# Turning the FFN's gated product on VectorE and by SBUF transfers instead of on TensorE

## The reference

```python
h2 = rms_norm(x, g_pre_ffn[l]) * (1 + scale_f) + shift_f
f = (jax.nn.silu(h2 @ w_ffn_gate[l]) * (h2 @ w_ffn_up[l])) @ w_ffn_down[l]
x = x + gate_f * rms_norm(f, g_post_ffn[l])
```

## Time and profile before

| | before |
|---|---|
| time, median of 3 runs | 2398.11 us (2397.22 to 2399.67) |
| span of the profiled execution | 2395.4 us |
| mean granted TensorE clock | 0.999 |
| PE, busy share of the span | 99% |
| DVE, busy share | 67% |
| ACT, busy share | 47% |
| POOL, busy share | 0% |
| FFN, gate and up product | about 698 to 1163 us of the span |

### The profile page before, as it was taken

The page is one execution under the profiler, slowest core; times in us unless marked ns, Lnnn a source line. Parts: engine busy times, 40 slices in busy tenths (PEclk is TensorE's granted clock), DMA queues, the critical chain, the costliest instruction groups (busy, mean ns, idle before and its releaser), DMA issues.

```text
span 2395.4 us, 31219 instructions
## 1 busy us (share of the span) xinstructions
PE 2379.1 (99%) x11027; PEld 1973.6 (82%) x11027; DVE 1594.5 (67%) x1962; ACT 1120.6 (47%) x1415; POOL 9.8 (0%) x18
## 2 busy tenths in 40 slices
PE   8999999999999999999999999999999999999998
PEld 7888788888888888888888888888888888888887
DVE  7998899899787765444444465446654557777664
ACT  4544545544464444444444454445544444444554
POOL 0001000000000000000000000000000000000000
PEclk9999999999999999999999999999999999999999
DMA  9986479999768875555655555655555554444454
GB/s 392 384 313 209 155 265 352 331 343 366 294 202 273 281 245 192 188 180 197 207 193 193 193 193 180 210 201 184 201 192 187 183 194 158 148 167 155 157 190 159
DMA packets 148490, 539.32 MB, mean 225 GB/s; under 512 B 16768, under 2 KB 18080, under 8 KB 147744
## 3 DMA queue, kind: packets, MB, share of 16 engines
q1 hardware_dynamic: 145584, 528.28, 64.4%
q10 hardware_dynamic: 2800, 9.59, 1.1%
HBM read 535.69 MB, written 2.11 MB: 225 GB/s over the span
## 4 chain that ended last, share of the span: by engine, by line
PE 98%; DVE 1%; DMA 1%; ACT 0%; issue 0%; SPq 0%; ACTq 0%; DVEq 0%
PE acc L1970 29%; PE acc L1972 29%; PE acc L1971 29%; PE tb L2052 2%; PE tb L2509 1%; DMA start_raw<-in_wa_dram 1%; PE tb L1970 1%; PE tb L1971 0%; PE tb L1972 0%; PE acc L2022 0%; PE acc L2021 0%; PE acc L2020 0%; PE tb L2512 0%; PE tb L2239 0%; PE acc L2031 0%; DVE macc L1340 0%
## 5 line engine op out<-in xcount | busy, mean ns | idle before, releaser
L1149 DVE TENSOR_TENSOR lo<-raw,hi 128x1024 fp32r<-128x1024 f32 x809 | 968.2, 1208 | 596.8 <-ACT hi L566 595.0
L566 ACT ACTIVATE hi<-raw 128x1024 fp32r<-128x1024 f32 x809 | 842.1, 1049 | 900.4 <-PE acc L1972 705.5
L1970 PE MATMUL acc<-hi,Hh 128*128 128x512 f32 x1960 | 775.4, 396 | 1.2 <-DVE Hl L1692 0.7
L1972 PE MATMUL acc<-hi,Hl 128*128 128x512 f32 x1960 | 764.3, 390 | 0.0
L1971 PE MATMUL acc<-lo,Hh 128*128 128x512 f32 x1960 | 763.1, 389 | 0.0
L1970 PEld LDWEIGHTS acc<-hi,Hh 128*128 128x128 f32 x1960 | 368.1, 188 | 79.0 <-issue 4.4
L1972 PEld LDWEIGHTS acc<-hi,Hl 128*128 128x128 f32 x1960 | 367.9, 188 | 77.7
L1971 PEld LDWEIGHTS acc<-lo,Hh 128*128 128x128 f32 x1960 | 368.4, 188 | 75.5 <-issue 1.4
L1970 PE MATMUL acc<-hi,hbh 128*128 128x512 f32 x512 | 204.8, 400 | 0.0
L1972 PE MATMUL acc<-hi,hbl 128*128 128x512 f32 x512 | 200.1, 391 | 0.0
L1971 PE MATMUL acc<-lo,hbh 128*128 128x512 f32 x512 | 199.6, 390 | 0.0
(11 more groups left out here) (325 smaller groups left out, 1966.5 us busy)
## 6 DMA issues: line engine op xcount, KB each, us to landing
raw<-in_wa_dram SPq DMA_DIRECT2D x680, 512.0 KB, 4.3
late_raw<-in_wa_dram SPq DMA_DIRECT2D x96, 512.0 KB, 5.4
raw<-in_wb_dram SPq DMA_DIRECT2D x96, 512.0 KB, 3.4
start_raw<-in_wa_dram SPq DMA_DIRECT2D x64, 512.0 KB, 7.8
raw<-in_wc_dram SPq DMA_DIRECT2D x64, 512.0 KB, 4.2
x<-in_x_dram SPq DMA_DIRECT2D x2, 1024.0 KB, 6.1
gm<-gate_rows ACTq DMA_DIRECT2D x2, 1024.0 KB, 8.2
x<-in_x_dram ACTq DMA_DIRECT2D x1, 2048.0 KB, 9.2
```

Of the source, the lines that this page charges most:

```text
L566: act.activation(hi[:, s, 0:n], raw[:, r, 0:n], ACT.Copy).then_inc(hi_ready, 1)
L1149: dve.tensor_tensor(lo[:, s, 0:n], raw[:, r, 0:n], hi[:, s, 0:n].bitcast(F32), ALU.subtract)\
L1970: pe.matmul(dst(tt), a, hi[:, s, w], start=first and i == 0, stop=False)
L1972: mm = pe.matmul(dst(tt), b, hi[:, s, w], start=False, stop=last and i == kts - 1)
```

## The change

The product in `tok` is no longer turned by PE. DVE turns the 32 x 32 blocks of each token tile (two `STREAM_TRANSPOSE` instructions from `tok` into `sgt`), which leaves each block in the wrong group of 32 partitions. POOL then issues sixteen SBUF to SBUF transfers of 32 partitions x 256 float32 (32 KB, rows of 1 KB), one for each pair of groups, from `sgt` back into `tok`. ACT and DVE take `hidh` and `hidl` from `tok` instead of from `tb`, in `hidden_hi` and `hidden_lo`. All of it waits on four new semaphores: `hid_blocks` (DVE to POOL), `hid_turned` (the transfers to ACT, 256 for each hidden tile), `hid_hi` (ACT to DVE), `hid_split` (DVE to PE, before the down product's first unit and before its unit 20).

```diff
+        blocks_out = sgt[:].rearrange("p a (j m) -> p (a j) m", j=2)
+        blocks_in = tok[:, 0].rearrange("p a (i m) -> p (a i) m", i=2)
+        def turned_half(tt):
+            return blocks_in[:, :, tt * P:(tt + 1) * P].rearrange("p i (k t) -> p k i t", k=4)
...
@@ gpsimd
+            for n in range(FT):
+                pool.wait_ge(hid_blocks, n + 1)
+                for i in range(4):
+                    for j in range(4):
+                        pool.dma_start(blocks_in[32 * j:32 * j + 32, i, :], blocks_out[32 * i:32 * i + 32, j, :])\
+                            .then_inc(hid_turned, 16)
@@ scalar
-            def hidden(n, first=8):
+            def hidden_hi(n, turned):
+                act.wait_ge(hid_turned, turned)
+                for tt in range(TT):
+                    act.activation(hidh[:, cols(n * 4, 4), tt * P:(tt + 1) * P].rearrange("p k (i t) -> p k i t", i=4),
+                                   turned_half(tt), ACT.Copy).then_inc(hid_hi, 1)
+            def hidden(first=5):
                 split(first)
                 tile_done()
                 read_out(lambda tt: sgt[:, tt, :], 0, ACT.Silu)
-                split(8)
-                take_hi_tile(hidh, n * 4)
+                split(11)
...
             for n in range(1, FFN_MOD):
-                hidden(n)
+                hidden_hi(n - 1, 256 * n)
+                hidden()
@@ vector
-            def hidden(n, units=16):
-                split(units - 2)
+            def hidden_lo(n, taken):
+                for tt in range(TT):
+                    dve.wait_ge(hid_hi, taken + tt + 1)
+                    at = slice(tt * P, (tt + 1) * P)
+                    four = lambda ap: ap.rearrange("p k (i t) -> p k i t", i=4)
+                    ins = dve.tensor_tensor(four(hidl[:, cols(n * 4, 4), at]), turned_half(tt),
+                                            four(hidh[:, cols(n * 4, 4), at].bitcast(F32)), ALU.subtract)
+                ins.then_inc(hid_split, 1)
+            def hidden(units=10):
+                split(units)
                 tile_done(2)
                 for tt in range(TT):
                     dve.tensor_tensor(tok[:, 0, tt, :], acc[:, 2 + tt, :], sgt[:, tt, :], ALU.mult).then_inc(acc_free[2 + tt], 1)
-                split(2)
-                take_lo_tile(hidl, hidh, n * 4)
+                n = c.up("hidden")
+                for tt in range(TT):
+                    dve.wait_ge(acc_free[2 + tt], n + (TILES_BEFORE_OUT // 2 + 3))
+                for tt in range(TT):
+                    ins = dve.transpose(blocks_out[:, :, tt * P:(tt + 1) * P].rearrange("p j (k t) -> p j k t", k=4),
+                                        tok[:, 0, tt, :].rearrange("p (k j c) -> p j k c", k=4, j=4))
+                ins.then_inc(hid_blocks, 1)
+                split(6)
@@ tensor
             def next_hidden():
-                def hidden():
-                    read_out(1)
-                    transpose_tok(0, tr_split)
-                tile(Hh, Hl, 0, 8, after={1: hidden})
+                tile(Hh, Hl, 0, 8)
                 tile(Hh, Hl, 1, 8)
...
                 if t == 0:
-                    tile(hidh, hidl, 0, FK // 2, before={FK // 2 - 2: split_now}, after={1: last_hidden})
+                    tile(hidh, hidl, 0, FK // 2, before={i: (lambda n=n: pe.wait_ge(hid_split, n)) for i, n in ((0, FT - 1), (FK // 2 - 2, FT))},
+                         after={1: lambda: gate_rows_out(1)})
```

More of the change, by code:

```diff
@@ L367, in two_blocks @@
         tr_copy = sem("tr_copy")
+        hid_blocks = sem("hid_blocks")
+        hid_turned = sem("hid_turned")
+        hid_hi = sem("hid_hi")
+        hid_split = sem("hid_split")
         uv_summed = sem("uv_summed")
@@ L910, in hidden @@
                 read_out(lambda tt: sgt[:, tt, :], 0, ACT.Silu)
-                split(8)
-                take_hi_tile(hidh, n * 4)
-            hidden(0, FFN0 + 12 - c.n["unit"])
+                split(11)
+            hidden(FFN0 + 12 - c.n["unit"])
             for n in range(1, FFN_MOD):
-                hidden(n)
-            with c.loop(act, FT - FFN_MOD, unit=16, raw=16, split=2) as n:
-                hidden(n + FFN_MOD)
+                hidden_hi(n - 1, 256 * n)
+                hidden()
+            with c.loop(act, FT - FFN_MOD, unit=16, raw=16) as n:
+                hidden_hi(n + (FFN_MOD - 1), n * 256 + 256 * FFN_MOD)
+                hidden()
+            hidden_hi(FT - 1, 256 * FT)
             store_gate(1)
-            split(4)
+            split(1)
             load_gate(gm2, 1)
@@ L1718, in hidden @@
                     dve.tensor_tensor(tok[:, 0, tt, :], acc[:, 2 + tt, :], sgt[:, tt, :], ALU.mult).then_inc(acc_free[2 + tt], 1)
-                split(2)
-                take_lo_tile(hidl, hidh, n * 4)
-            hidden(0, FFN0 + 20 - c.n["unit"])
+                n = c.up("hidden")
[6 more added lines that the diff above has]
+                split(6)
+            hidden(FFN0 + 18 - c.n["unit"])
             for n in range(1, FFN_MOD):
-                hidden(n)
+                hidden_lo(n - 1, TT * (n - 1))
+                hidden()
             add_bias(GATE_F, KD)
             gated_gain(GATE_F, "g_post_ffn")
-            with c.loop(dve, FT - FFN_MOD, unit=16, raw=16, hi=2) as n:
-                hidden(n + FFN_MOD)
+            with c.loop(dve, FT - FFN_MOD, unit=16, raw=16, hidden=1) as n:
+                hidden_lo(n + (FFN_MOD - 1), n * TT + TT * (FFN_MOD - 1))
+                hidden()
+            hidden_lo(FT - 1, TT * (FT - 1))
             for t in range(3):
-                split(FK // 2 - (t == 0))
+                split(FK // 2 - (5 if t == 0 else 0))
                 gated_tile(fmix, gm2, t % 2, t * N)
@@ L2401, in _ @@
                 next_hidden()
-            with c.loop(pe, FT - FFN_MOD, unit=16, raw=16, acc0=1, acc1=1, tb0=1, tb1=1):
+            with c.loop(pe, FT - FFN_MOD, unit=16, raw=16, acc0=1, acc1=1):
                 next_hidden()
[L2405 to L2408, removed]
             for t in range(4):
                 if t == 0:
-                    tile(hidh, hidl, 0, FK // 2, before={FK // 2 - 2: split_now}, after={1: last_hidden})
+                    tile(hidh, hidl, 0, FK // 2, before={i: (lambda n=n: pe.wait_ge(hid_split, n)) for i, n in ((0, FT - 1), (FK // 2 - 2, FT))},
+                         after={1: lambda: gate_rows_out(1)})
                 elif t < 3:
```

## The result

| | before | changed |
|---|---|---|
| time, median of 9 runs | 2397.58 us (2396.95 to 2399.67) | 2403.79 us (2402.63 to 2406.20) |
| ratio to before, 95% interval | | 1.0027 (1.0017 to 1.0036) |
| span of the profiled execution | 2395.4 us | 2404.4 us |
| mean granted TensorE clock | 0.999 | 0.997 |

The change costs 6.2 us, 0.27%. I forecast 2389 us. The page of the changed kernel: span, busy times, the chain that ended last, DMA queues (packets, MB, share), and the new transfers (KB, median us to landing).

What follows compares the result with a forecast made beforehand. PE, busy 99% of the span, was taken to bound the kernel. Span 2395.4 - 9.8 (transposes) + 1.0 (added in tiles 0 to 3) = 2386.6, plus 2.7 for the runs' median, gave 2389 us; range 2386 to 2450.

Steps and rivals of the forecast that it cites:

- the last landing w: Time from the last of POOL's sixteen transfers being issued to its landing; taken as 2 us, 4 beside modulation blocks.
- What bounds the kernel: Claim that the time is the sum of what PE runs: busy 99% of the span, 98% of the last-ending chain.
- what PE gives up: Eight PE transposes per turned hidden tile, claimed to cost 0.89 us; eleven tiles give 9.8 us off the path.
- The deadline: Latest last landing before PE waits for unit 23: 15.5 us after DVE's product starts; 14.6 in tiles 0 to 3.
- T: When a hidden tile's last transfer lands, from the start of DVE's product; forecast 12.7 us, 14.7 in tiles 0 to 3.
- t: Time in us within a hidden tile, counted from the start of DVE's product.
- The issue pitch d: Time between POOL's issues of the sixteen transfers, called the main unknown; taken as 0.5 us, range 0.45 to 1.5.
- S: PE's stall per hidden tile, T - 15.5 us where positive; at 0.89 us it eats up the gain.
- just late: Rival: chain slightly late, pitch 0.70 to 0.75 us or landing 4 us everywhere; 2393 to 2402 us, chance 0.10.
- my last sign of being wrong: Forecast is wrong if DMA load holds the small transfers back by more than 2.8 us over what was taken.
- What else is added: Extra cost of DVE's block transposes ahead of modulation blocks and unit 18 in tiles 0 to 3: 1 us in all.
- a slow issue: Rival: POOL issues the sixteen transfers slowly; at a pitch of 0.9 us the time is 2428 us, chance 0.28.

Runs made afterwards that it cites:

- the kernel with quiet loads: The changed kernel with SP's weight loads from the FFN on cut to a quarter of their width (128 KB instead of 512): 2387.24 us, one run.

## Why the prediction was wrong

I forecast 2389 us and a gain; measured were 2403.79 us and a loss. The step that failed first is the last landing w, which I put at 2 us and which was 5.6. Two more things came on top: I charged too little for what is added in tiles 0 to 3, and I did not foresee a late start of POOL.

**What bounds the kernel, and what PE gives up**: right. The 0.89 us per tile is there, 43.52 us wherever nothing is late, and the kernel turned the new way in seven tiles got 5.4 of the 6.2 us that seven tiles should give.

**The deadline**: right to 0.4 us. I had T = 15.5 for unit 23. Landings at t = 14.9 lost nothing, at 15.1 0.05 us (the kernel with quiet loads, tile 8), at 15.7 0.5, at 15.9 0.8 and at 16.2 1.0, so it lies at 15.1 to 15.2. Part of the difference is the 0.14 us from the landing to `hidh`, which my sum left out.

**The issue pitch d**: I named it the main unknown, took 0.5 us and hung the rivals on it. It was 0.49 us (498 ns for each of 176). The block transposes were as taken too, 1.30 us for the pair. The Trainium skill's 1 us to the first byte ("DMA: Bandwidth & Descriptors", "Latency and other measured facts") was not paid sixteen times: the first transfer of a burst landed 1.7 us after its issue, and the next was issued 0.49 us behind it.

**The last landing w**: this step failed. I took 2 us, for a single small transfer on fairly quiet engines, and 4 for loaded ones only in tiles 0 to 3, from the earlier trace rows. It was 5.6 in tile 7, and 5.2 is the median of all 176. Within the burst of tile 7 the landing grows from 1.7 us for the first transfer to 5.2 for the seventh and stays at 5.2 to 5.9 after that. It takes both the crowd and the loads: beside the full loads one transfer alone lands after 1.7 us, and the last of sixteen after 5.6; with the loads cut to a quarter the last of sixteen lands after 1.7 in tiles 4 to 10.

The trace of the kernel before held nearer rows. Of the five small transfers that gave me the pitch, two are of exactly 32 KB:

```profile
iropeC<-in_table_dram ACTq DMA_DIRECT2D x1, 32.0 KB, 7.5
iropeS<-in_table_dram ACTq DMA_DIRECT2D x1, 32.0 KB, 7.3
```

They were issued one behind another beside loads of about 400 GB/s, and landed after 7.3 to 7.5 us. I took the pitch from this group and not the landing.

The Trainium skill ("DMA: Bandwidth & Descriptors", "Anatomy of one DMA", the GpSimd path) gives a fixed 2.0 us plus the bytes at 436 GB/s; for 32 KB that is 2.1 us, an estimate from that page. The median of the quiet kernel, 2.1, agrees, and that of the change is 3 us above it.

With w = 5.6 my own sum gives T = 1.3 + 1.3 + 0.1 + 8 + 5.6 = 16.3. Measured was 15.9: POOL started at 3.0 and not at 2.7, and the last issue is 15 pitches behind the first, 7.3 us and not 8. So S is 0.8 by my deadline, eleven tiles lose about as much as PE gives up, and the change is close to nothing from these terms. This is the rival that I called "just late" and gave 0.10. It named both ways there, a pitch above 0.7 or a landing of 4 us everywhere, and it was the second; and my last sign of being wrong, small transfers held back by more than 2.8 us over what I took, is what came (3.6 us). The measured time still lies above that rival's 2402, because of the next two points.

**What else is added**: mis-sized. I charged 1 us for tiles 0 to 3. They lost 6.7 us in the change and 6.9 with the wait out of the way, so there the late landing is not what costs. PE's largest wait in each of these tiles stood at t = 17, in front of unit 22, which ACT makes before it waits for the transfers, and not at unit 24. I had added up whether the `lo` of unit 18 comes in time (PE wants it at t = 5.2, not at the 5.1 that I wrote), and it did but for 0.3 us in tile 1; I had not followed the slots. DVE's 1.3 us stand in front of a modulation block, the block's `raw` slot is given back 1.4 us later, SP's next load goes out that much later, and the burst of transfers then slows the loads. DVE's order costs nothing without the burst, and both together cost nothing beside quiet loads. Beside full loads the burst costs 2.1 to 3.2 us with two units in front of the transposes and 7 us with the transposes in front.

**The late start in tile 8**: not foreseen. POOL's 3.1 us moved the last landing to t = 18.3. As the chain had no margin this cost 4.8 us, three quarters of the whole result: 3.2 us of PE's wait, and 1.6 us at the lower clock behind it.

By the table of pitches the tiles lost 16.5 us where I had charged 1. Of the 15.5 us between, about 6 belong to the landing (tiles 4 to 10, with 0.8 of tile 8's loss), about 6 to tiles 0 to 3, and 4 to the late start.

**The range** began at 2386 and reached 2450, so it held the time, but by luck: it reached up there for a slow issue, which did not happen. The chances spoke for the wrong side: lateness needed a pitch above 0.67 us only as long as w was 2. At w = 5.6 it needs 0.45.

## What to carry to other kernels

A chain of many small transfers has two prices, the issue pitch and the landing of the last one. Take the second from rows where as many are in flight beside the same load; here it was three times what a lone transfer showed. Put the wait for such a chain as late as the data allows: here four units later turned +6.2 us into -3.6. Where loads are scarce, an instruction that stands between a buffer's last use and its release is paid by the load behind it, so put new work behind the release: that took the gain from 3.6 to 7.5 us and gave the best version, 2389.7 us.

## What the hardware showed that I had not expected

- Transfers of 32 KB issued by POOL every 0.49 us landed 1.7 us after issue at first and 5.6 us at the sixteenth, beside loads of about 190 GB/s; 2.1 us at the median where all traffic was 60 to 78 GB/s. A lone one beside the full loads landed after 1.7 us. Halving the bytes took off 1.1 us.
- POOL's 129th transfer was issued 3.1 us late, in each kernel that has one.
- In tile 8 PE stood idle for 2.9 us, and behind that its granted clock fell to the lower level for about 3.4 us, which cost 1.6 us more. Tile 8 of the kernel with 48 memsets shows the same (0.53 from 1103.0 to 1106.2 us).
- ACT needed 0.65 us to issue each of sixteen such transfers and did nothing else in that time, 10.4 us a burst.
- The `STREAM_TRANSPOSE` of 128 x 512 float32 takes 0.69 us, as long as a product of the same size.
